# High and low parts of the weights word by word in one array, on one core of a Trainium2 chip

## The chip, the cores and the metric

The kernel runs on 1 core of one Trainium2 chip. The metric is the device time in microseconds of one execution on that core, as the median of several runs. Less is better.

## What is computed

The reference is two transformer blocks in float32, one after the other, on 256 tokens of width 1024. The first block also reads 256 context tokens; the second adds 16 meta tokens in front. Cut to what matters:

```python
# first block
px = modulate(rms_norm(x, g_pre_mix), sh_m, sc_m) @ w_in        # x: 256 x 1024, w_in: 1024 x 2320
pc = modulate(rms_norm(ctx, g_pre_mix), csh_m, csc_m) @ w_in
mixed = concat(attention(...), mlstm_output(...))               # window attention and a two-way mLSTM
x = x + gt_m * rms_norm(mixed @ w_out, g_post_mix)
x = x + gt_f * rms_norm(swiglu(modulate(rms_norm(x, g_pre_ffn), sh_f, sc_f), w_ffn_in, w_ffn_out), g_post_ffn)
# second block, h = [16 meta tokens, x]
h = h + 0.5 * swiglu_2(rmsnorm(h, ffn1_norm), ffn1_w_gate, ffn1_w_up, ffn1_w_down)     # hidden width 2816
u = rmsnorm(h, mix_norm) @ w_in_2                                                      # attention, GLA, gates
h = h + (sigmoid(gate_a) * (ya @ w_branch_att) + sigmoid(gate_b) * (yb @ w_branch_gla)) @ w_out_2
h = h + 0.5 * swiglu_2(rmsnorm(h, ffn2_norm), ffn2_w_gate, ffn2_w_up, ffn2_w_down)
out = rmsnorm(h, final_norm)[:, 16:]
```

Nearly all of the arithmetic is products of a weight matrix with 256, 258, 272 or 512 token columns.

## The kernel before

Every weight tile comes from HBM in float32 and is used in two parts, a high one rounded to the matmul type `F32R` and a low one that is the rest. A product then takes three matmuls: high weight times high activation, high weight times low activation, low weight times high activation (`split_mm`, lines 2003 to 2007, and copies of it at 2134, 2203 to 2205 and 2398).

The weights run through a ring of four slots (`RING` = 4). Each slot holds up to 1408 words in every partition (`SLOT`); most tiles are 1024 words (four row blocks of 256 columns), those of the down projections 1408 (eleven row blocks of 128 columns). Three arrays of four slots stand next to each other: `raw` takes the transfer from HBM, which SyncE issues (line 419); ScalarE copies `raw` to `hi` (line 621); VectorE subtracts, `lo = raw - hi` (line 1143); TensorE reads `hi` and `lo`. The order of the slots is fixed: ScalarE waits for TensorE's count of finished slots (`mm_done`) before it overwrites `hi`, VectorE waits for ScalarE, TensorE for VectorE, and SyncE's next transfer into `raw` for VectorE. All of this runs a slot or more ahead of TensorE.

```python
hi = sbuf(root, "hi", [P, RING, SLOT], F32R)                                                  # 137
lo = sbuf(root, "lo", [P, RING, SLOT], F32R)                                                  # 138
act.activation(hi[:, j, 0:width], raw[:, j, 0:width], ACT.Copy).then_inc(hi_ready, 1)         # 621
dve.tensor_tensor(lo[:, j, 0:width], raw[:, j, 0:width], hi[:, j, 0:width].bitcast(F32), ...) # 1143
pe.matmul(out_, wH, xH, start=start, stop=False)                                              # 2005
pe.matmul(out_, wH, xL, start=False, stop=False)                                              # 2006
return pe.matmul(out_, wL, xH, start=False, stop=stop)                                        # 2007
pe.matmul(out_, n5H[:, k, rows], hi[:, k // 2, w], start=k == 0, stop=False)                  # 2203
pe.matmul(out_, n5H[:, k, rows], lo[:, k // 2, w], start=False, stop=False)                   # 2204
return pe.matmul(out_, n5L[:, k, rows], hi[:, k // 2, w], start=False, stop=k == KD - 1)      # 2205
pe.matmul(bank, hi[:, 0, 0:P], hi[:, 0, 0:512], start=True, stop=True)                        # 2480
```

In `pe.matmul(out, a, b)` the second argument is the stationary operand, which a separate LDWEIGHTS instruction (PEld in the profile) brings into the array; the third is the moving operand, which streams past it, one column per clock at best. So the weights are stationary in `split_mm`: 128 words of `hi` or `lo` for each LDWEIGHTS. They are the moving operand in two places only. One is `by_token` (lines 2203 to 2205), used for the mLSTM's values and output gates (phases `winv` and `wino` of the first block): 48 calls of three matmuls, each with 512 words of `hi` or `lo` moving, 12 matmuls to a piece; the pieces are laid between the steps of the attention (`scores`, `probabilities`, `values_out`). The other is `keep_clock` (line 2480), which multiplies to no purpose while TensorE waits for a norm: 7 matmuls before `gu0`, 16 before `gu1`, 4 and 3 at the end of the kernel, each with 512 words of `hi` moving.

The phases in order: `win0`, `winq`, `winm`, `winv`, `wino` (products with `w_in`, beside attention and mLSTM), `wout`, `gu0` and `dn0` (first feed-forward, 11 and 4 turns of four slots), `gu1` and `dn1`, `in2k` and `in2g`, `brb` and `bra`, `wout2`, `gu2` and `dn2`. TensorE, VectorE, ScalarE and SyncE run a turn of the feed-forwards in hardware loops.

Of the kernel before, what the change touches and what calls it, by code (L numbers as in the profile page):

```python
# [7 lines left out]
F32R = mybir.dt.float32r  # L8
# [6 lines left out]
P = 128  # L15
# [13 lines left out]
SLOT = HALF * P  # L29
RING = 4  # L30
# [84 lines left out]
def program(nc, dr, out):  # L115
    with ExitStack() as root:
        def sbuf(stack, name, shape, dt=F32):
            return stack.enter_context(nc.sbuf_tensor(name, shape, dt))
# [15 lines left out]
        slabs1 = ExitStack()  # L134
        slab_hi = sbuf(slabs1, "slab_hi", [P, RING, SLOT])
        slabs1.close()
        hi = sbuf(root, "hi", [P, RING, SLOT], F32R)
        lo = sbuf(root, "lo", [P, RING, SLOT], F32R)
        sinkn = sbuf(root, "sinkn", [P, 16])
        negm = sbuf(root, "negm", [P, 32])  # L140
        staged = ExitStack()
# [2653 lines left out]
```

## Time and profile before

| | us |
|---|---|
| median of 3 runs | 971.9 (969.46 to 973.7) |
| the profiled execution's own time | 973.39 |
| span of the profiled execution | 971.6 |
| TensorE (matmul) busy | 956.6, 98% of the span |
| weight load (PEld) busy | 888.0, 91% |
| VectorE busy | 641.1, 66% |
| ScalarE busy | 495.0, 51% |

The span runs from the first to the last instruction on the chip; the execution's own time has some 2 us more around it. A matmul's duration in the profile includes its passage through the array, and matmuls overlap: what one costs TensorE is the distance from its start to the next start, which is shorter than its duration. The same holds for weight loads. The mean granted clock of TensorE is 0.994 of full speed.

### The profile page before, as it was taken

What the parts mean: (1) busy time and instruction counts of PE and PEld (TensorE: products, weight loads), DVE (VectorE), ACT (ScalarE), POOL (GpSimd) and SP (SyncE); (2) the same over time, 40 slices, a digit from 0 to 9 for tenths busy, and PEclk for the clock granted to TensorE, in tenths of its full rate; (3) what the DMA queues carried; (4) which work ended last, traced back from release to release, by engine and by line L of the source; (5) the groups of instructions that cost most, each with busy time, mean ns of one, the idle gap of its engine ahead of it and who ended that gap; (6) DMA issues with size and microseconds to landing.
All of it is one profiled execution on the core that took longest, in us unless ns stands there. A gap on an engine that the chain in (4) does not pass through costs nothing.

```text
span 971.6 us, 19403 instructions
## 1 busy us (share of the span) xinstructions
PE 956.6 (98%) x7543; PEld 888.0 (91%) x7543; DVE 641.1 (66%) x990; ACT 495.0 (51%) x762; POOL 66.6 (7%) x100
## 2 busy tenths in 40 slices
PE   8999999999999999999999999999999999999997
PEld 3776778899999999899999999999999999999997
DVE  4788886687666765765555546665778766665654
ACT  3755647655444544554444434645566555444540
POOL 0012002200000021000000000200210100000000
PEclk9999998999999999999999999999999999999999
DMA  9982447547556696266666844663445566667841
GB/s 346 384 283 88 131 131 231 163 172 216 173 174 182 191 308 177 71 197 173 176 177 183 217 119 129 212 188 108 131 131 173 154 194 204 184 177 220 217 120 43
DMA packets 189183, 176.06 MB, mean 181 GB/s; under 512 B 7312, under 2 KB 177824, under 8 KB 188752
## 3 DMA queue, kind: packets, MB, share of 16 engines
q1 hardware_dynamic: 183456, 154.29, 53.9%
q0 software_dynamic: 4960, 17.64, 5.3%
q10 hardware_dynamic: 720, 3.49, 0.9%
q8 instruction: 31, 0.51, 0.2%
q14 instruction: 16, 0.13, 0.0%
HBM read 174.32 MB, written 1.05 MB: 180 GB/s over the span
## 4 chain that ended last, share of the span: by engine, by line
PE 87%; DVE 8%; ACT 2%; issue 1%; DMA 1%; POOL 0%; DVEq 0%; ACTq 0%; POOLq 0%
PE acc L2005 23%; PE acc L2006 23%; PE acc L2007 23%; PE acc L2398 3%; DVE lo L1143 2%; PE acc L2101 1%; DMA stage<-in_w_late 1%; PE acc L2203 1%; PE acc L2205 1%; PE acc L2204 1%; PE wk L2064 1%; PE wk L2005 1%; PE wk L2006 1%; PE wk L2007 1%; PE wk L2134 1%
## 5 line engine op out<-in xcount | busy, mean ns | idle before, releaser
L1143 DVE TENSOR_TENSOR lo<-raw,hi 128x1024 fp32r<-128x1024 f32 (+1 forms) x259 | 331.5, 1291 | 208.0 <-ACT hi L621 207.7
L621 ACT ACTIVATE hi<-raw 128x1024 fp32r<-128x1024 f32 (+1 forms) x260 | 283.8, 1099 | 133.5 <-PE acc L2007 114.7
L2005 PE MATMUL acc<-n_high,hi 128*128 128x272 f32 (+3 forms) x1016 | 290.5, 286 | 0.5 <-DVE hbuf L1671 0.3
L2006 PE MATMUL acc<-n_low,hi 128*128 128x272 f32 (+3 forms) x1016 | 289.2, 285 | 0.0
L2007 PE MATMUL acc<-n_high,lo 128*128 128x272 f32 (+3 forms) x1016 | 288.1, 284 | 0.0
L2005 PEld LDWEIGHTS acc<-n_high,hi 128*128 128x128 f32 (+1 forms) x1016 | 191.4, 188 | 3.1 <-issue 1.4
L2006 PEld LDWEIGHTS acc<-n_low,hi 128*128 128x128 f32 (+1 forms) x1016 | 191.0, 188 | 0.5
L2007 PEld LDWEIGHTS acc<-n_high,lo 128*128 128x128 f32 (+1 forms) x1016 | 191.0, 188 | 0.2
L2005 PE MATMUL acc<-g_high,hi 128*128 128x256 f32 (+1 forms) x528 | 148.9, 282 | 0.9 <-DVE lo L1143 0.9
L2006 PE MATMUL acc<-g_low,hi 128*128 128x256 f32 (+1 forms) x528 | 149.1, 282 | 0.0
L2007 PE MATMUL acc<-g_high,lo 128*128 128x256 f32 (+1 forms) x528 | 148.7, 282 | 0.0
L2005 PE MATMUL acc<-mixH,hi 128*128 128x256 f32 x400 | 112.9, 282 | 0.5 <-DVE gab L1844 0.4
L2006 PE MATMUL acc<-mixL,hi 128*128 128x256 f32 x400 | 112.1, 280 | 0.0
L2007 PE MATMUL acc<-mixH,lo 128*128 128x256 f32 x400 | 112.1, 280 | 0.0
L2005 PEld LDWEIGHTS acc<-g_high,hi 128*128 128x128 f32 x528 | 99.3, 188 | 1.2 <-DVE lo L1143 1.1
L2007 PEld LDWEIGHTS acc<-g_high,lo 128*128 128x128 f32 x528 | 99.9, 189 | 0.0
L2006 PEld LDWEIGHTS acc<-g_low,hi 128*128 128x128 f32 x528 | 99.1, 188 | 0.0
L2006 PEld LDWEIGHTS acc<-mixL,hi 128*128 128x128 f32 x400 | 76.5, 191 | 0.0
L2005 PEld LDWEIGHTS acc<-mixH,hi 128*128 128x128 f32 x400 | 75.1, 188 | 1.5 <-DVE gab L1844 0.7
L2007 PEld LDWEIGHTS acc<-mixH,lo 128*128 128x128 f32 x400 | 75.1, 188 | 0.0
L566 POOL TENSOR_TENSOR sq<-sq 128x256 f32<-128x256 f32 (+1 forms) x28 | 23.8, 851 | 482.7 <-ACT sq L923 431.0
L923 ACT ACTIVATE sq<-R (+3 forms) x36 | 15.9, 441 | 57.6 <-DVE R L1715 49.9
(424 smaller groups left out, 1254.5 us busy)
## 6 DMA issues: line engine op xcount, KB each, us to landing
raw<-in_w_in SPq DMA_DIRECT2D x52, 512.0 KB, 3.8
raw<-in_w_ffn_in SPq DMA_DIRECT2D x44, 512.0 KB, 3.9
raw<-in_ffn_w_gate SPq DMA_DIRECT2D x44, 512.0 KB, 3.9
raw<-in_ffn_w_up SPq DMA_DIRECT2D x44, 512.0 KB, 3.8
raw<-in_ffn_w_down SPq DMA_DIRECT2D x32, 704.0 KB, 4.8
stage<-in_w_late POOLq DMA_DIRECT2D x24, 512.0 KB, 5.4
raw<-in_w_ffn_out SPq DMA_DIRECT2D x16, 704.0 KB, 6.2
raw<-in_w_out SPq DMA_DIRECT2D x16, 512.0 KB, 3.6
```

What stands on the lines that cost most here:

```text
L566: ins = pool.tensor_tensor(sq[:, 0, 0:width], sq[:, 0, 0:width], sq[:, k, 0:width], ALU.add)
L621: act.activation(hi[:, j, 0:width], raw[:, j, 0:width], ACT.Copy).then_inc(hi_ready, 1)
L923: act.activation(sq[:, k, 0:width], R[:, k, t0:t0 + width], ACT.Square).then_inc(sq_ready, 1)
L1143: dve.tensor_tensor(lo[:, j, 0:width], raw[:, j, 0:width], hi[:, j, 0:width].bitcast(F32), ALU.subtract).then_inc(lo_ready, 1)
L2005: pe.matmul(out_, wH, xH, start=start, stop=False)
L2006: pe.matmul(out_, wH, xL, start=False, stop=False)
L2007: return pe.matmul(out_, wL, xH, start=False, stop=stop)
L2064: ins = pe.matmul(SLAB_BANK[n][32 * kk:32 * kk + 32, :], silu_c[:, 4 * q + kk, :], SLAB_MEM[n][2 * q + kk // 2][:, 512 * (kk % 2):512 * (k ...
L2101: pe.matmul(acc[:, 0, 0:width], cink[:, 0, 0, 0:P], cink.rearrange("p a b t -> p (a b t)")[:, 0:width], start=True, stop=True)
L2134: ins = pe.matmul(bank[:, T * m:T * m + T], ws[:, j, w], xs[:, k, 0:T], start=k == 0 and m == 0 and n == 0, stop=k == KD - 1 and n == 2, s ...
L2203: pe.matmul(out_, n5H[:, k, rows], hi[:, k // 2, w], start=k == 0, stop=False)
L2398: ins = pe.matmul(out_, ws[:, j, w], xs[:, k, :], start=k == 0 and m == 0 and n == 0, stop=k == KD - 1 and n == 2, skip_group_check=True)
```

## The change

The two arrays `hi` and `lo` are replaced by one of the same total size in which the words alternate: high, low, high, low. The names `hi` and `lo` become views of it, so every read and write of either steps over two words (8 bytes) where it took adjacent words (4 bytes) before. No instruction, semaphore or transfer is added, removed or moved, and `raw` stays as it is. The arrays allocated after these two keep their addresses. `slab_hi` (line 135), a temporary array that lies where `hi` begins, now lies under the high and low words of slots 0 and 1 and no longer under the high words of all four.

```diff
@@ -134,8 +134,8 @@
         slabs1 = ExitStack()
         slab_hi = sbuf(slabs1, "slab_hi", [P, RING, SLOT])
         slabs1.close()
-        hi = sbuf(root, "hi", [P, RING, SLOT], F32R)
-        lo = sbuf(root, "lo", [P, RING, SLOT], F32R)
+        weights = sbuf(root, "weights", [P, RING, SLOT, 2], F32R)
+        hi, lo = weights[:, :, :, 0], weights[:, :, :, 1]
         sinkn = sbuf(root, "sinkn", [P, 16])
         negm = sbuf(root, "negm", [P, 32])
         staged = ExitStack()
```

## Rows read from the trace of the kernel before

**Rows 1.** The page: span, busy time by engine, slices of the span
```profile
span 971.6 us, 19403 instructions
PE 956.6 (98%) x7543; PEld 888.0 (91%) x7543; DVE 641.1 (66%) x990; ACT 495.0 (51%) x762; POOL 66.6 (7%) x100
...
PEclk9999998999999999999999999999999999999999
```

**Rows 2.** The chain that ended last, whole span, shares by line
```profile
by line: PE acc L2005 23.2%; PE acc L2006 22.9%; PE acc L2007 22.8%; PE acc L2398 2.6%; DVE lo L1143 1.6%; issue 1.3%; PE acc L2101 1.1%; DMA stage<-in_w_late 1.0%; PE acc L2203 1.0%; PE acc L2205 0.9%; PE acc L2204 0.9%; PE wk L2064 0.8%; 
```

**Rows 3.** Groups by line and shape: splits (count, busy us, mean ns, idle before)
```profile
L1143 DVE TENSOR_TENSOR lo<-raw,hi 128x1024 fp32r<-128x1024 f32 x207 | 252.3, 1229 | 153.0 <-ACT hi L621 152.8
L621 ACT ACTIVATE hi<-raw 128x1024 fp32r<-128x1024 f32 x208 | 217.2, 1051 | 86.8 <-PE acc L2007 84.6 <-DMA raw<-in_w_in 1.8
...
L1143 DVE TENSOR_TENSOR lo<-raw,hi 128x1408 fp32r<-128x1408 f32 x48 | 77.9, 1634 | 54.3 <-ACT hi L621 54.2
...
L621 ACT ACTIVATE hi<-raw 128x1408 fp32r<-128x1408 f32 x48 | 65.7, 1375 | 46.7 <-PE acc L2007 30.1 <-DMA raw<-in_w_ffn_out 12.5 <-DMA raw<-in_ffn_w_down 3.7
```

**Rows 4.** Line 2005's weight loads: duration min/median/max; 16 and 128 words
```profile
L2005 PEld LDWEIGHTS acc<-g_high,hi x528: 186/188/190, 329.0 to 961.7; 128*128 128x128 f32 x176
...
L2005 PEld LDWEIGHTS wk<-n5H,hi x8: 92/94/98, 65.6 to 70.2; 128*16 128x16 f32 x8
```

**Rows 5.** Timeline of TensorE: start and duration us, 512 moving words of weights
```profile
105.20 0.39 PE L2203 MATMUL acc<-hi,n5H 128*128 128x512 f32 x1
105.43 0.40 PE L2204 MATMUL acc<-lo,n5H 128*128 128x512 f32 x1
...
107.07 0.40 PE L2205 MATMUL acc<-hi,n5L 128*128 128x512 f32 x1
```

**Rows 6.** The same in `dn0` and `dn2`: 256 moving words of activations
```profile
350.04 0.28 PE L2005 MATMUL acc<-g_high,hi 128*128 128x256 f32 x1
...
351.40 0.28 PE L2005 MATMUL acc<-g_high,hi 128*128 128x256 f32 x1
...
899.91 0.28 PE L2005 MATMUL acc<-g_high,hi 128*128 128x256 f32 x1
...
900.97 0.28 PE L2005 MATMUL acc<-g_high,hi 128*128 128x256 f32 x1
```

**Rows 7.** Groups of TensorE from 89.8 to 145.5 us
```profile
L2203 PE MATMUL acc<-hi,n5H 128*128 128x512 f32 x48 | 20.1, 419 | 0.0
L2205 PE MATMUL acc<-hi,n5L 128*128 128x512 f32 x48 | 18.9, 395 | 0.0
L2204 PE MATMUL acc<-lo,n5H 128*128 128x512 f32 x48 | 18.9, 394 | 0.0
L2254 PE MATMUL wk<-cst,Sm 128*128 128x128 f32 x48 | 7.0, 279 | 0.5 <-DVE Sm L1446 0.4
```

**Rows 8.** Windows: busy us of each engine (instructions), granted clock, DMA
```profile
89.80:100.60 10.80, 10.80 (x73) 8.05 (x70) 10.55 (x27) 3.93 (x8) 0.46 (x2) 1.00 0.17 51
100.60:144.90 44.30, 43.82 (x249) 31.64 (x249) 36.09 (x78) 25.78 (x49) 4.25 (x12) 1.00 0.45 143
```

**Rows 9.** Timeline around `keep_clock` before `gu0`, before `gu1`, at the end
```profile
197.38 1.86 PE L2480 MATMUL acc<-hi 128*128 128x512 f32 x7
...
199.57 0.36 PE L2005 MATMUL wk<-n_high,hi 128*128 128x258 f32 x1 [0.33 <-DVE n_low L1647]
...
391.15 4.00 PE L2480 MATMUL acc<-hi 128*128 128x512 f32 x16
...
395.99 0.37 PE L2005 MATMUL wk<-n_high,hi 128*128 128x272 f32 x1 [0.84 <-DVE n_low L1647]
...
962.55 1.17 PE L2480 MATMUL acc<-hi 128*128 128x512 f32 x4
...
963.85 0.61 PE L2738 MATMUL wk<-cst,sq 128*128 128x1 f32 x4
...
964.31 0.94 PE L2480 MATMUL acc<-hi 128*128 128x512 f32 x3
...
965.43 0.70 PE L2742 MATMUL wk<-xg,cst 128*128 128x256 f32 x2 [0.18 <-DVE xg L1990]
```

**Rows 10.** Windows, columns as in rows 8: a turn of `gu0`, of `gu1`
```profile
228.50:240.10 11.60, 11.60 (x98) 11.60 (x98) 8.16 (x13) 5.54 (x8) 0.00 (x0) 1.00 0.66 206
...
460.00:472.00 12.00, 12.00 (x98) 12.00 (x98) 6.90 (x7) 5.43 (x8) 0.00 (x0) 1.00 0.64 175
```

**Rows 11.** Groups by shape: TensorE's matmuls with a stationary `hi`, by moving words
```profile
L2005 PE MATMUL acc<-n_high,hi 128*128 128x272 f32 x400 | 115.0, 287 | 0.3 <-DVE hbuf L1671 0.3
L2005 PE MATMUL acc<-mixH,hi 128*128 128x256 f32 x400 | 112.9, 282 | 0.5 <-DVE gab L1844 0.4
L2005 PE MATMUL acc<-g_high,hi 128*128 128x256 f32 x352 | 98.2, 279 | 0.9 <-DVE lo L1143 0.9
L2005 PE MATMUL acc<-n_high,hi 128*128 128x258 f32 x336 | 95.4, 284 | 0.0
...
L2005 PE MATMUL acc<-n_high,hi 128*128 128x256 f32 x272 | 77.6, 285 | 0.3 <-DVE n_low L1956 0.3
```

## The prediction

> **What bounds the kernel now.** I read the page first: TensorE is busy 956.6 of 971.6 us at a granted clock of 0.9 or more in every slice [rows 1]. VectorE at 66% and ScalarE at 51% have room on average. The chain that ended last says the same: lines 2005 to 2007 hold 69% of it, while VectorE's split of the weights holds 1.6% [rows 2]. So what the change does to TensorE's reads counts first, and what it does to the two splitting engines counts only once they run late.
>
> The change touches nothing but the distance between words, so the next thing to read is how fast each engine takes words today. Four readers or writers of `hi` and `lo` are concerned.
> - TensorE's moving stream: eight steps of 512 words take 107.07 - 105.20 = 1.87 us, 234 ns each [rows 5]. That is 0.457 ns per word, or 8.8 bytes per ns in every partition. At 2.4 GHz the array itself would want 213 ns, so the stream runs 10% behind it although TensorE waits for nothing there. With 256 words, 12 steps of `dn0` take 1.36 us, 113 ns each, and 9 of `dn2` take 1.06 us, 118 ns each [rows 6]: 0.44 to 0.46 ns per word again. A turn of `gu0` is 96 matmuls of 258 words in 11.6 us, 121 ns each, one of `gu1` 96 of 272 words in 12.0 us, 125 ns each [rows 10].
> - The weight load: 188 ns for 128 words, 94 ns for 16 words [rows 4], so 94 / 112 = 0.84 ns per word; 128 words occupy it for 107 ns, 4.8 bytes per ns.
> - ScalarE's split: (1375 - 1051) / 384 = 0.84 ns per word [rows 3].
> - VectorE's split: (1634 - 1229) / 384 = 1.05 ns per word [rows 3].
>
> **The change part by part.** No row of this trace shows an operand with a step of two words. I therefore compare the stretch of memory that each stream sweeps per ns with the fastest sweep that a row shows, 8.8 bytes per ns, that of the moving stream. Stepped by 8 bytes, VectorE's streams sweep 8 / 1.05 = 7.6 bytes per ns, below it; the weight load and ScalarE sweep 8 / 0.84 = 9.5, 8% above it; the moving stream would have to sweep 17.7, twice it. By this measure three of the four keep their pace or nearly so, and the fourth cannot be promised to.
>
> (a) Moving reads of 512 weight words in `by_token`. There are 3 x 48 = 144 of them [rows 7]. Bounds: nothing, if a stepped read costs the same; 234 ns each, if 512 words with gaps cost what 1024 adjacent words would (256 to 512 words adds 234 - 116 = 118 ns [rows 5, 6], so another 512 words add some 236). I take the upper end, because this stream is the only one that moves two words in the time of one weight-load word, and it already runs behind the clock. Sum: 144 x 234 = 33.7 us. Does it land? From 89.8 to 144.9 us TensorE is busy 10.80 + 43.82 of 55.1 us [rows 8], and its only wait for another engine is 0.4 us for a softmax step at line 2254 [rows 7]. TensorE works in order, so these matmuls push all that follows: 33.3 us land. The chain gives lines 2203 to 2205 2.8%, 27 us [rows 2]; the missing 6 us belong to 90 to 104 us, where VectorE is 98% busy [rows 8] and the chain runs through it. That cover is used up: with TensorE's pieces 2.8 us longer each, VectorE's steps fit in them. Below nothing: I see no reason for a gain here.
>
> (b) Moving reads in `keep_clock`, 30 matmuls, doubled to 468 ns. Before `gu0` 7 x 234 = 1.6 us start at 197.38 and end near 199.0; the next product waits for VectorE until 199.57 [rows 9]. Doubled they end near 200.6, 1.1 us late. Before `gu1` 16 x 234 = 3.7 us end near 394.9 and become 7.5, ending near 398.6 where 395.99 was the start: 2.6 us late, of which the later waits of that front may give back some; I take 2. At the end 4 become 1.87 us and end at 964.4, 0.55 us after 963.85; then 3 of 468 ns end at 966.3, where line 2742 would start at 965.43 + 0.55: 0.3 more. Together 1.1 + 2 + 0.85 = 4 us; bounds 0 and 4.6.
>
> (c) Weight loads from `hi` and `lo`. Lines 2005 to 2007 have 2016 loads of 128 words each (the sum of their groups, of which the largest stand in [rows 11]), lines 2134 and 2398 another 336: about 6,400. A load overlaps the matmul before it; it occupies 107 ns where starts are 113 to 125 ns apart. If it holds its 0.84 ns per word, nothing changes. If it is held to the sweep of 8.8 bytes per ns, it takes 128 x 8 / 8.8 = 116 ns, and with the 6 ns that now lie between load and pace in `dn0`, 122 ns. The 256-word matmuls at 113 to 118 ns would then go at 122 (+4 to 9 ns, some 3,400 of them), those of 258 words from 121 to 122, those of 272 words not at all: about 22 us. Upper bound: each word costs like two, 188 + 107 = 295 ns of duration and 214 ns of occupation, so starts 220 ns apart, +100 ns x 6,400 = 640 us. I take nothing, because the load is within 8% of a sweep that the rows show, and keep 22 us for the range.
>
> (d) The splits. If stepped words cost them nothing: 0. If each cost like two: VectorE 1.05 x 1024 = +1.07 us, ScalarE +0.86 us. In a turn of `gu0` VectorE has 8.16 of 11.6 us of work and four splits [rows 10]: 8.16 + 4.3 = 12.4, just over the turn; in `gu1` 6.90 + 4.3 = 11.2 of 12.0 fits. On the chain VectorE's splits have 1.6%, 15.5 us or some 13 splits [rows 2, 3]: 13 x 1.07 = 14 us, and 11 turns of `gu0` add up to 9 us. Today's cover in the loops is the idle time before the splits, 153 us before VectorE's [rows 3]. I take nothing: 7.6 bytes per ns lies below the shown sweep, and ScalarE's 8% more (0.07 us a split) is hidden by that idle time.
>
> (e) Addresses: the sum of the sizes is the same, so what is allocated behind keeps its place, and the one transfer that lands there (`slab_hi`, before the first split) keeps its waits. Nothing.
>
> Sum against the profiled execution: 973.4 + 33.3 + 4 = 1010.7 us; that execution lies 1.5 us above the median, so against the median 971.9 + 37 = **1009 us**.
>
> **The skill against the rows.** The rows show one word per 0.457 ns moving and one per 0.84 ns loading [rows 4, 5], both of adjacent words, and decide nothing on steps. The Trainium skill, page "Advanced Engine Details and Errata", section "SBUF Cachelines", says that accesses get full performance as long as at least two fall on a 16-byte line. Two words of a view that steps by 8 bytes do; by that rule all of (a) to (d) is nothing and the time stays at 972, which is the first rival. Against it the page "Vector Engine (DVE) Microarchitecture Reference", section 5.2, asks for runs of two adjacent words and gives about 1.7 ns per word where there are none; by that VectorE's split would take 0.65 ns more per word, toward the last two rivals. Its table tells of steps other than two words, so neither rule is shown here.
>
> **The rivals.**
> - Not slower, 972 us: the memory hands TensorE a piece wide enough that every second word of it still feeds one word per 0.45 ns. Place: lines 2203 to 2205. Price: none. It decides if starts stay 234 ns apart; any stretch above 240 ns speaks against it. For it: the 9% lag behind the array is there with stationary weights too, and may have nothing to do with reading.
> - Weight loads just too slow as well, 1009 + 22 = 1031 us, from (c). For it: the load has 6 to 11 ns of slack and must sweep 8% faster than anything shown.
> - Every stepped word costs like two: 1009 + 640 = about 1650 us, and TensorE is bound by its loads. For it: the upper bounds above; against it: three of the four sweeps stay near a shown one.
> - Only the splits suffer, TensorE not: 972 + 14 + 9 = 995 us at most.
> - Faster: equal products in `dn0` and `dn2` differ by 4.4 ns [rows 6], for a reason the rows don't show. If another order of words made all 256-word matmuls go at 113 ns and those of 258 words at 114, 1,600 x 4.4 + 1,056 x 6.6 ns = 14 us would go: 958 us.
> - That the change does nothing of what it says is excluded for the reads: the views are stepped. A stepped operand may be built into the same instructions, as a step is part of each operand.
>
> **How the numbers follow.** Moving stream doubled, rest unchanged: 0.42. Not slower: 0.27. Loads just too slow: 0.12. Everything doubled: 0.12. Splits alone: 0.03. Faster: 0.04. The likeliest gives 1009. The range takes in the unchanged case from below, 968, and the case of the slower loads with room for twice its size above 1009, 1060; the doubled case and the faster one, 0.16, stay out. About 0.5%, 5 us, is what a measurement here can tell from no change. Faster by more 0.04; within 0.27; slower by more 0.42 + 0.12 + 0.12 + 0.03 = 0.69.
>
> **What would show it.** Right: starts near 468 ns apart at lines 2203 to 2205, their stretch 33 us longer, `keep_clock` of 16 taking 7.5 us; weight loads at 188 ns and starts in `gu0`, `gu1` and `dn2` at 121, 125 and 118 ns; splits at 1.05 and 1.23 us. Wrong: starts still at 234 ns, or weight loads above 200 ns with the whole feed-forward stretched, or a VectorE split near 1.9 us.

## The result, and the profile after

The changed kernel takes 1019.0 us (median of 4 runs, 1018.2 to 1021.3) against 971.5 us before (four runs; the three that stood ahead of the prediction had 971.9): a ratio of 1.0503, 95% interval 1.0478 to 1.0529, so 47.6 us slower. The forecast was 1009 us in a range of 968 to 1060. Its direction and range held; 10 of the 47.6 us were missing from the likeliest case.

The page of the changed kernel, beside [rows 1], and its chain by line, beside [rows 2] (both of the arrays are called `weights` now):

```profile
span 1019.5 us, 19403 instructions
PE 1007.2 (99%) x7543; PEld 908.6 (89%) x7543; DVE 641.1 (63%) x990; ACT 519.3 (51%) x762; POOL 68.0 (7%) x100
...
by line: PE acc L2005 23.8%; PE acc L2007 23.1%; PE acc L2006 23.0%; PE acc L2398 2.5%; PE acc L2203 2.3%; PE acc L2205 2.1%; PE acc L2204 2.1%; PE acc L2480 1.4%; DMA slab_hi<-in_w_ada 1.1%; PE wk L2005 0.8%; PE wk L2007 0.8%; PE wk L2006 
```

The same 19403 instructions, and the chain's new time lies in TensorE's lines. Lines 2203 to 2205, where weights are the moving operand, went from 2.8% to 6.5% of the chain; `keep_clock` (line 2480) has appeared with 1.4%; VectorE's busy time is to the tenth what it was. Its splits, 1.6% of the chain before, no longer stand among the chain's largest lines. That TensorE is now late enough to cover them is how I read it.

The timeline of TensorE at the end of `wino` (start and duration in us), beside [rows 5]:

```profile
173.45 0.65 PE L2205 MATMUL acc<-weights,n5L 128*128 128x512 f32 x1
173.90 0.65 PE L2203 MATMUL acc<-weights,n5H 128*128 128x512 f32 x1
174.36 0.65 PE L2204 MATMUL acc<-weights,n5H 128*128 128x512 f32 x1
174.81 0.64 PE L2205 MATMUL acc<-weights,n5L 128*128 128x512 f32 x1
175.38 1.10 PE L2359 MATMUL acc<-vtok,kw 128*64 128x129 f32 x16
```

512 moving words now take 1.36 / 3 = 453 ns from start to start, where they took 234. In `dn0`, beside [rows 6], the moving operand is still adjacent words of activations and only the stationary one is stepped:

```profile
381.82 0.28 PE L2005 MATMUL acc<-g_high,weights 128*128 128x256 f32 x1
...
383.26 0.28 PE L2005 MATMUL acc<-g_high,weights 128*128 128x256 f32 x1
```

12 steps in 1.44 us: 120 ns each instead of 113. Not doubled, but 7 ns more, in a place where nothing but TensorE's own pace counts. The weight loads beside [rows 4] and the splits beside [rows 3]:

```profile
L2005 PEld LDWEIGHTS acc<-g_high,weights x528: 193/193/202, 362.3 to 1008.9; 128*128 128x128 f32 x176
...
L1143 DVE TENSOR_TENSOR weights<-raw,weights 128x1024 fp32r<-128x1024 f32 x207 | 252.2, 1229 | 166.4 <-ACT weights L621 165.9
L621 ACT ACTIVATE weights<-raw 128x1024 fp32r<-128x1024 f32 x208 | 235.8, 1147 | 82.9 <-PE acc L2007 80.4 <-DMA raw<-in_w_in 2.3
...
L621 ACT ACTIVATE weights<-raw 128x1408 fp32r<-128x1408 f32 x48 | 72.2, 1511 | 44.6 <-PE acc L2007 31.2 <-DMA raw<-in_w_ffn_out 9.8 <-DMA raw<-in_ffn_w_down 3.2
```

A load takes 193 to 196 ns instead of 188; ScalarE's split of 1024 words 1147 ns instead of 1051; VectorE's split, which now reads and writes stepped words, takes 1229 ns as before.

To see where the 47.6 us arose I set the start of the same matmul in both traces side by side (the n-th of the 7543 that each trace holds) and took the growth of the difference over each stretch:

| stretch of the program | later by, us |
|---|---|
| up to the first piece of `winv` | -0.4 |
| `winv` and `wino` | +30.4 |
| from there to `keep_clock` before `gu0` (mostly `wout`) | +1.2 |
| `keep_clock` of 7, 16 and 4 + 3 matmuls | +1.0, +2.6, +0.8 |
| `gu0` and `dn0` | +4.5 |
| `gu1` and `dn1` | -0.5 |
| `in2k` to the end of the attention of the second block | +3.5 |
| from there through `dn2` | +5.0 |

So three terms: moving reads in `winv` and `wino` 30.4, `keep_clock` 4.4, and 13 to 14 us spread over all products with stationary weights. The last is the one that the forecast had at nothing. In `gu0`, with 258 moving words, 800 matmuls lose 0.9 us, 1.1 ns each; in `gu2` and `dn2`, with 256, 1,200 lose 2.6 us, 2.2 ns each.

### The profile page after: what moved, and what is told of

Read it like the earlier page. It is cut to its first block, busy times and chain, and to the rows that moved or that the text cites. A ratio compares the mean times of both kernels' runs of the same rounds, so it can differ in the third digit from the quotient of the medians.

```text
span 1019.5 us, 19403 instructions
## 1 busy us (share of the span) xinstructions
PE 1007.2 (99%) x7543; PEld 908.6 (89%) x7543; DVE 641.1 (63%) x990; ACT 519.3 (51%) x762; POOL 68.0 (7%) x100
## 3 DMA queue, kind: packets, MB, share of 16 engines
HBM read 174.32 MB, written 1.05 MB: 172 GB/s over the span
## 4 chain that ended last, share of the span: by engine, by line
PE 93%; DVE 3%; ACT 1%; DMA 1%; issue 1%; SPq 0%; DVEq 0%; ACTq 0%
PE acc L2005 24%; PE acc L2007 23%; PE acc L2006 23%; PE acc L2398 3%; PE acc L2203 2%; PE acc L2205 2%; PE acc L2204 2%; PE acc L2480 1%; DMA slab_hi<-in_w_ada 1%; PE wk L2005 1%; PE wk L2007 1%; PE wk L2006 1%; PE wk L2246 1%; PE acc L2134 1%; PE wk L2268 1%
## 5 line engine op out<-in xcount | busy, mean ns | idle before, releaser
L1143 DVE TENSOR_TENSOR weights<-raw,weights 128x1024 fp32r<-128x1024 f32 (+1 forms) x259 | 331.7, 1291 | 225.5 <-ACT weights L621 225.1
L621 ACT ACTIVATE weights<-raw 128x1024 fp32r<-128x1024 f32 (+1 forms) x260 | 308.9, 1201 | 127.4 <-PE acc L2007 111.6
L2005 PE MATMUL acc<-n_high,weights 128*128 128x272 f32 (+3 forms) x1016 | 293.8, 289 | 0.4 <-DVE hbuf L1671 0.4
L2006 PE MATMUL acc<-n_low,weights 128*128 128x272 f32 (+3 forms) x1016 | 289.9, 285 | 0.0
L2007 PE MATMUL acc<-n_high,weights 128*128 128x272 f32 (+3 forms) x1016 | 289.8, 285 | 0.0
L2005 PEld LDWEIGHTS acc<-n_high,weights 128*128 128x128 f32 (+1 forms) x1016 | 198.4, 195 | 2.7 <-issue 1.4
L2006 PEld LDWEIGHTS acc<-n_low,weights 128*128 128x128 f32 (+1 forms) x1016 | 198.4, 195 | 0.4
L2007 PEld LDWEIGHTS acc<-n_high,weights 128*128 128x128 f32 (+1 forms) x1016 | 197.9, 195 | 0.2
L2005 PE MATMUL acc<-g_high,weights 128*128 128x256 f32 (+1 forms) x528 | 150.6, 285 | 0.7 <-DVE weights L1143 0.7
L2007 PE MATMUL acc<-g_high,weights 128*128 128x256 f32 (+1 forms) x528 | 150.2, 285 | 0.0
L2005 PE MATMUL acc<-mixH,weights 128*128 128x256 f32 x400 | 113.9, 285 | 0.5 <-DVE gab L1844 0.5
L2007 PE MATMUL acc<-mixH,weights 128*128 128x256 f32 x400 | 113.0, 283 | 0.0
L2005 PEld LDWEIGHTS acc<-g_high,weights 128*128 128x128 f32 x528 | 102.4, 194 | 0.9 <-DVE weights L1143 0.9
L2007 PEld LDWEIGHTS acc<-g_high,weights 128*128 128x128 f32 x528 | 102.6, 194 | 0.0
L2005 PEld LDWEIGHTS acc<-mixH,weights 128*128 128x128 f32 x400 | 77.3, 193 | 1.3 <-DVE gab L1844 0.7
L2007 PEld LDWEIGHTS acc<-mixH,weights 128*128 128x128 f32 x400 | 77.6, 194 | 0.0
```

## The experiments

The theory going in: the step between words costs, once for each kind of read, and the kinds add up. The rivals: it is not the step but the place (high and low parts of a slot close together, so that engines meet in the same memory), or the slower splits of ScalarE, and not TensorE's own reads. The code cuts below show the lines that matter; like edits of other lines are left out.

**One array without a step.** In each slot first all high words, then all low ones. `Words(array, part, g)` is a view of one part (0 high, 1 low): with `g` None the parts lie one behind the other, with a number they alternate in runs of `g` words:

```diff
-        hi = sbuf(root, "hi", [P, RING, SLOT], F32R)
-        lo = sbuf(root, "lo", [P, RING, SLOT], F32R)
+        weights = sbuf(root, "weights", [P, RING, 2 * SLOT], F32R)
+        hi, lo = Words(weights, 0, None), Words(weights, 1, None)
```

> One array again, as in the change, but in each slot first all high words and then all low words, so that every view steps by one word. Theory 1, the step is what costs: the time is that of the kernel before, 971 us within 3, loads 188 ns, 512 moving words 234 ns apart, ScalarE's split of 1024 words 1.05 us. Theory 2, it is the place (high and low parts of a slot close together, so that engines meet in the same stretch of memory): it stays well above 971, up to 1019 us. Theory 3: an array with the slots side by side changes the 113 or 118 ns between starts of equal products: up to 14 us faster.

Measured: 970.5 us against 970.2, ratio 1.0002 (0.9981 to 1.0023). High and low parts share one slot's stretch of memory as in the change, the addresses of everything else are the same, and nothing is lost. So the place is not the cause at the scale of a slot; the runs of four words below, where the parts lie 16 bytes apart, say the same of small distances for the moving reads. What remains is the step. Nor was anything gained. All later layouts are built on this one.

**The moving reads put back**, first those of `winv` and `wino`, then those of `keep_clock` too. The split and `by_token` take their words from the layout without a step in these phases:

```diff
+        hi, lo = Words(weights, 0, 1), Words(weights, 1, 1); hiT, loT = Words(weights, 0, None), Words(weights, 1, None)
-                act.activation(hi[:, j, 0:width], raw[:, j, 0:width], ACT.Copy).then_inc(hi_ready, 1)
+                act.activation((hiT if isinstance(g, int) and g in (BASE["winv"], BASE["wino"]) else hi)[:, j, 0:width], raw[:, j, 0:width], ACT.Copy).then_inc(hi_ready, 1)
-                pe.matmul(out_, n5H[:, k, rows], hi[:, k // 2, w], start=k == 0, stop=False)
+                pe.matmul(out_, n5H[:, k, rows], hiT[:, k // 2, w], start=k == 0, stop=False)
```

and, in the second kernel only,

```diff
-                    pe.matmul(bank, hi[:, 0, 0:P], hi[:, 0, 0:512], start=True, stop=True)
+                    pe.matmul(bank, weights[:, 0, 0:P], weights[:, 0, 0:512], start=True, stop=True)
```

> The change, but in the phases winv and wino alone (mLSTM values and output gates, where weights are the moving operand) the slots hold all high words and then all low ones. Theory 1: starts at lines 2203 to 2205 are 234 ns apart again and the 30.5 us which the change lost between 90 and 145 us come back: 1019 - 30.5 = 988.5 us; the weight loads elsewhere stay at 195 ns. If those 30 us were lost to the slower splits or to VectorE's and ScalarE's steps of the attention beside it, little comes back in spite of 234 ns.

> As the one before, and keep_clock reads adjacent words too, so that only weight loads and splits step by two words. Theory 1: keep_clock gives back 4 to 5 us: 984 us. The remaining 12 us are those of the weight loads: starts in dn0 stay near 120 ns, in gu0 122, in dn2 120. If keep_clock's length is hidden by the norm beside it: 988 us as before.

Measured: 989.4 us, ratio 1.0194 (1.0163 to 1.0225), and 986.8 us, ratio 1.0164 (1.0131 to 1.0196). The first gives back 1019.0 - 989.4 = 29.6 us where 30.5 was expected; in its trace lines 2203 to 2205 start 232 ns apart again in the middle, and `winv` and `wino` are 30.4 us shorter than in the change. Their splits are without a step here too; that these are not what gave the time back shows in the kernel with stepped splits alone, below. The second gives 2.6 us more where I had 4 to 5. In the traces, `keep_clock` costs the first kernel 1.1 + 2.6 + 0.7 = 4.4 us against the kernel before and the second nothing, so the medians and the traces agree only within their spread of some 2 us. What is left, 16 us with 13 to 19 in its interval (13.2 in the trace), has no stepped moving read in it.

**The prices alone.** A kernel that does nothing of the reference's work but copy an input, and runs each spacing by itself: 16 matmuls with 512 moving words from an array with one stationary operand of adjacent words, then 24 matmuls each with stepped stationary words, then ScalarE and VectorE alone.

> None of the reference's work but the copy of an input: each price alone. 16 matmuls of 512 moving words for each spacing (every word, every 2nd, 3rd, 4th, 8th, and runs of 2, 4, 8, 16 words with as many left out), 24 matmuls of 256 and of 128 moving words for each spacing of the 128 stationary words (1, 2, 3, 4, 8), then ScalarE and VectorE alone with 1024 words. Theory 1a, memory is read in pieces of 16 bytes at one rate: moving 512 words take 230, 455, 680, 900, 900 ns; runs of 2 take 455 like every 2nd word, runs of 4, 8 and 16 take 230. Theory 1b, pieces of 8 bytes: 230, 455, 455, 455, 455, and runs of 2 take 230 already. Loads with every word or every 2nd take 107 to 114 ns of TensorE's time, with every 4th word and above about 225 by theory 1a, 114 by 1b. ScalarE's write of every 2nd word: 0.94 ns per word as in the kernel, every 4th 1.8 by theory 1a. VectorE: 1.05 ns up to every 2nd word, every 4th 1.7 to 1.8 by theory 1a, 1.05 by 1b.

Its timeline of TensorE, each line one spacing; the price of one is the distance to the start of the next line by the count. Lines 124 to 132: every word, every 2nd, 3rd, 4th, 8th as moving operand; 134 and 136: runs of 2 and of 4 words with as many left out. Line 150: every 8th of the stationary words beside 256 moving words. Lines 152 to 158: 128 stationary words, every one, every 2nd, 3rd, 4th, beside 128 moving words.

```profile
30.11 3.79 PE L124 MATMUL acc<-mov,sta 128*128 128x512 f32 x16
33.73 7.41 PE L126 MATMUL acc<-mov,sta 128*128 128x512 f32 x16
40.97 7.38 PE L128 MATMUL acc<-mov,sta 128*128 128x512 f32 x16
48.16 7.57 PE L130 MATMUL acc<-mov,sta 128*128 128x512 f32 x16
55.54 7.08 PE L132 MATMUL acc<-mov,sta 128*128 128x512 f32 x16
62.44 7.40 PE L134 MATMUL acc<-mov,sta 128*128 128x512 f32 x16
69.66 3.91 PE L136 MATMUL acc<-mov,sta 128*128 128x512 f32 x16
73.41 3.89 PE L138 MATMUL acc<-mov,sta 128*128 128x512 f32 x16
...
96.50 5.96 PE L150 MATMUL acc<-mov,sta 128*128 128x256 f32 x24
102.29 2.79 PE L152 MATMUL acc<-mov,sta 128*128 128x128 f32 x24
104.92 2.99 PE L154 MATMUL acc<-mov,sta 128*128 128x128 f32 x24
107.75 4.32 PE L156 MATMUL acc<-mov,sta 128*128 128x128 f32 x24
111.91 5.82 PE L158 MATMUL acc<-mov,sta 128*128 128x128 f32 x24
117.52 5.78 PE L160 MATMUL acc<-mov,sta 128*128 128x256 f32 x24
```

Moving: 3.62 / 16 = 226 ns for adjacent words, then 452, 449, 461, 431 for every 2nd, 3rd, 4th and 8th, 451 for runs of 2, and 3.75 / 16 = 234 for runs of 4. Both forms of theory 1 fall for the moving operand. By pieces of 16 bytes at one rate every 3rd and 4th word should have cost 680 and 900; by pieces of 8 bytes runs of 2 should have been free. It has two prices only: 0.44 to 0.46 ns per word in runs of four, 0.84 to 0.90 otherwise, however far apart.

Loads: with 128 moving words TensorE has less to stream than to load, so these are the loads' own prices: 2.63 / 24 = 110 ns for adjacent words, 118 for every 2nd, 173 for every 3rd, 234 for every 4th. That is 64, 96 and 128 pieces of 16 bytes at 1.84, 1.81 and 1.83 ns each: here the 16-byte theory holds to 2%, and a step of two words is the last one that costs next to nothing. Every 8th word takes 5.79 / 24 = 241 ns, as much as every 4th to 3%: what counts is the number of pieces and not the stretch swept, by which it would have doubled.

ScalarE (lines 58 to 67: writing every word, every 2nd, 3rd, 4th; 70: every 8th) and VectorE (93 and 96: reading `hi` at every word and every 2nd; 99: every 4th; 111: reading and writing every 2nd), columns: count, busy us, mean ns, idle before:

```profile
L70 ACT ACTIVATE dst<-src 128x1024 fp32r<-128x1024 f32 x4 | 8.1, 2032 | 0.1
...
L67 ACT ACTIVATE dst<-src 128x1024 fp32r<-128x1024 f32 x4 | 8.0, 1998 | 0.1
...
L64 ACT ACTIVATE dst<-src 128x1024 fp32r<-128x1024 f32 x4 | 6.2, 1552 | 0.1
...
L61 ACT ACTIVATE dst<-src 128x1024 fp32r<-128x1024 f32 x4 | 4.5, 1116 | 0.1
...
L58 ACT ACTIVATE dst<-src 128x1024 fp32r<-128x1024 f32 x4 | 4.2, 1056 | 106.8 <-PE acc L162 106.7
...
L99 DVE TENSOR_TENSOR dst<-src,mov 128x1024 fp32r<-128x1024 f32 x4 | 7.9, 1971 | 0.1
...
L111 DVE TENSOR_TENSOR dst<-src,mov 128x1024 fp32r<-128x1024 f32 x4 | 4.9, 1226 | 0.1
L96 DVE TENSOR_TENSOR dst<-src,mov 128x1024 fp32r<-128x1024 f32 x4 | 4.9, 1226 | 0.1
L93 DVE TENSOR_TENSOR dst<-src,mov 128x1024 fp32r<-128x1024 f32 x4 | 4.9, 1225 | 175.5 <-ACT dst L84 175.4
```

The same 1.8 ns: with the 187 ns that [rows 3] leave beside 0.84 ns per word, ScalarE's 1116, 1552 and 1998 are 929 / 512, 1365 / 768 and 1811 / 1024 = 1.81, 1.78 and 1.77 ns per piece, and every 8th word costs what every 4th does (2032 ns). VectorE needs 2 x 1.05 = 2.1 ns for two words anyway, which is longer than a piece, which fits that every 2nd word costs it nothing, read and written. The Trainium skill, page "Advanced Engine Details and Errata", section "SBUF Cachelines", asks for two accesses to a 16-byte line; for VectorE, and nearly for the loads and ScalarE, the trace agrees (1226 ns against 1225, 118 against 110, 1116 against 1056). For the moving operand it does not: 452 ns against 226, with two words on every line.

**Loads alone and splits alone.** Two complements settle who owns the remaining 13 to 16 us. In the first, splits write adjacent words and TensorE's loads step by two over them; in the second, splits write every second word and TensorE reads adjacent ones. Both so multiply mixed words. `Load` and `Split` are views for reading and for writing, and the number behind each is its step:

```diff
+        hi, lo, hiW, loW, hiM, loM = (f(weights, q, s) for f, s in ((Load, 2), (Split, 1), (Load, 1)) for q in range(2))
-                act.activation(hi[:, j, 0:width], raw[:, j, 0:width], ACT.Copy).then_inc(hi_ready, 1)
+                act.activation(hiW[:, j, 0:width], raw[:, j, 0:width], ACT.Copy).then_inc(hi_ready, 1)
```

and `(Load, 1), (Split, 2)` in the other.

> Splits write adjacent words (all high ones, then all low ones), moving reads of weights take adjacent words, and only the weight loads step by two words; they so take a mixture of high and low words, and the products with stationary weights are not those of the reference. Theory 1, the 13 to 16 us that remained when the moving reads were put back are those of the loads: 985 to 987 us, starts in dn0 at 120 ns, weight loads at 193 to 196 ns. Theory 2, they come from the splits (ScalarE's write of a split 0.1 us longer, or engines meeting in memory): 971 us and loads at 188 ns.

> The counterpart: ScalarE and VectorE write every second word as in the change, and TensorE reads adjacent words everywhere, stationary and moving (so again mixed words, and other products). Theory 1: 971 us within 3, although ScalarE's split of 1024 words takes 1.15 us instead of 1.05, since VectorE waits for it with time to spare. Theory 2: up to 987 us.

Measured: loads stepped 986.0 us, ratio 1.0136 (1.0108 to 1.0164); splits stepped 971.5 us, ratio 0.9990 (0.9973 to 1.0006), both against 972.7 us in the same series. In the first, 256-word matmuls of `dn0` and `dn2` start 120 ns apart as in the change. From the groups by shape, first of the kernel with stepped loads, then of that with stepped splits:

```profile
L621 ACT ACTIVATE weights<-raw 128x1024 fp32r<-128x1024 f32 x208 | 217.1, 1052 | 94.1 <-PE acc L2007 91.2 <-DMA raw<-in_w_in 2.4
...
L2005 PEld LDWEIGHTS acc<-n_high,weights 128*128 128x128 f32 x1008 | 197.5, 196 | 2.4 <-issue 1.4 <-DVE hbuf L1671 0.5
```

```profile
L1143 DVE TENSOR_TENSOR weights<-raw,weights 128x1024 fp32r<-128x1024 f32 x207 | 252.4, 1229 | 155.4 <-ACT weights L621 154.9
L621 ACT ACTIVATE weights<-raw 128x1024 fp32r<-128x1024 f32 x208 | 233.5, 1136 | 77.3 <-PE acc L2007 74.8 <-DMA raw<-in_w_in 1.8 <-DMA raw<-in_ffn_w_up 0.6
L2005 PEld LDWEIGHTS acc<-n_high,weights 128*128 128x128 f32 x1008 | 190.6, 189 | 3.0 <-issue 1.4 <-DVE hbuf L1671 0.6 <-DVE n_low L1956 0.5
```

ScalarE at 1052 ns and loads at 196: 13 us slower. ScalarE at 1136 ns and loads at 189: not slower. The remainder belongs to the loads. ScalarE's 85 ns more per split are hidden whole: VectorE's idle time before its splits, 153 us before, is 155 us, and the total does not move. The stepped splits of `winv` and `wino` are among them, so those phases' 30 us are not theirs either.

**Moving reads alone, in single words, in runs of four and in runs of two.** High words and then low ones everywhere but in `winv` and `wino`, and there the parts alternate one by one, four by four, or two by two (the cut is that of four by four):

```diff
+        hi, lo = Words(weights, 0, None), Words(weights, 1, None); hiT, loT = Words(weights, 0, 4), Words(weights, 1, 4)
```

> High words and then low words in every slot but those of the phases winv and wino, where they alternate one by one; keep_clock takes adjacent words. If the losses add up independently: 971 + 30 = 1001 us, starts at lines 2203 to 2205 near 450 ns, weight loads at 188 ns and dn0 at 113 or 118 ns. If the moving reads cost less when the loads are fast: under 995.

> The same, but in winv and wino the parts alternate in runs of four words (16 bytes high, 16 bytes low). The prices measured alone say 233 ns for 512 words in runs of four with four left out: 971 us within 3. If what counts is the stretch of memory swept (8 KB for 2 KB of words, as with every second word): 1001 us.

> As the kernel with runs of four words in winv and wino, but in runs of two (8 bytes high, 8 bytes low). The prices measured alone say 451 ns for 512 words in runs of two, like every second word, and 233 ns in runs of four. So it should be as slow as with single words: 1001 to 1005 us. If two adjacent words were enough for the moving stream: 972 us.

Measured: single words 1004.8 us, ratio 1.0321 (1.0290 to 1.0351); runs of four 972.3 us, ratio 0.9991 (0.9970 to 1.0011); runs of two 1002.3 us, ratio 1.0302 (1.0258 to 1.0347). The timeline of TensorE with runs of four, then with runs of two:

```profile
105.28 0.39 PE L2204 MATMUL acc<-weights,n5H 128*128 128x512 f32 x1
...
106.67 0.40 PE L2204 MATMUL acc<-weights,n5H 128*128 128x512 f32 x1
```

```profile
105.36 0.64 PE L2204 MATMUL acc<-weights,n5H 128*128 128x512 f32 x1
105.81 0.63 PE L2205 MATMUL acc<-weights,n5L 128*128 128x512 f32 x1
...
106.72 0.63 PE L2204 MATMUL acc<-weights,n5H 128*128 128x512 f32 x1
```

1.39 / 6 = 232 ns against 1.36 / 3 = 453. Both sweep 4096 bytes for 2048 bytes of words (not the 8 KB that the expectation has), and one of them costs nothing: the stretch of memory swept is not what is paid for.

**More prices.** Does a run have to fill an aligned piece, and does a stepped load show beside every width of moving operand?

> Prices alone again, none of the reference's work but the copy of an input. Moving words: runs of four starting at a multiple of 16 bytes take 233 ns; starting 8 or 4 bytes later, 450 ns if a run has to fill one aligned piece of 16 bytes, 233 ns if only its length counts; runs of six of eight between the two (504 words, 340 ns); 512 adjacent words starting 4 or 8 bytes late 227 to 234 ns. Weight loads of adjacent and of every second word beside 256, 258, 272 and 512 moving words: with adjacent words 113 to 121, 114 to 121, 120 to 125 and 234 ns; with every second word 120, 120 to 122, 125 and 234 ns, no matter whether the first word is even (the high part) or odd (the low part): the load is the longer of the two up to 256 or 258 words and hidden above. ScalarE writes every second word at 0.85 to 0.9 ns, (1408 against 1024 words), the 0.94 ns of the kernel then being the meeting of engines.

Its timeline of TensorE. Lines 96, 98 and 100: runs of four of eight words, starting at a multiple of 16 bytes, 8 bytes late, 4 bytes late. 102: runs of six of eight (504 words). 104: runs of eight of sixteen, 8 bytes late. 106: 512 adjacent words, 4 bytes late. 110, 112 and 114: loads of adjacent words, of every 2nd and of every 2nd from an odd word on, beside 256 moving words; from line 116 on the same beside 258, then 272 and 512, of which the cut shows the first.

```profile
29.53 3.86 PE L96 MATMUL acc<-mov,sta 128*128 128x512 f32 x16
33.23 7.41 PE L98 MATMUL acc<-mov,sta 128*128 128x512 f32 x16
40.46 7.43 PE L100 MATMUL acc<-mov,sta 128*128 128x512 f32 x16
47.69 4.95 PE L102 MATMUL acc<-mov,sta 128*128 128x504 f32 x16
52.47 5.40 PE L104 MATMUL acc<-mov,sta 128*128 128x512 f32 x16
57.70 3.97 PE L106 MATMUL acc<-mov,sta 128*128 128x512 f32 x16
61.51 3.90 PE L108 MATMUL acc<-mov,sta 128*128 128x512 f32 x16
65.24 5.80 PE L110 MATMUL acc<-mov,sta 128*128 128x256 f32 x48
70.88 5.96 PE L112 MATMUL acc<-mov,sta 128*128 128x256 f32 x48
76.67 5.96 PE L114 MATMUL acc<-mov,sta 128*128 128x256 f32 x48
82.47 5.92 PE L116 MATMUL acc<-mov,sta 128*128 128x258 f32 x48
```

Runs of four: 231 ns aligned, 452 ns when they start 8 or 4 bytes late. Runs of six of eight: 4.78 / 16 = 299 ns. That is one aligned piece of four words at 1.8 ns and two single words at 0.88 each, 3.56 ns for six words, times 84 = 299: the two prices mix word by word. The expectation had 340 ns for it. Runs of eight starting 8 bytes late hold one aligned piece and four single words: the same sum gives 64 x (1.8 + 4 x 0.88) = 340 ns, and they took 327, which fits less well; the expectation had nothing on them. Adjacent words that start 4 bytes late lose next to nothing (238 ns).

Stepped loads beside 256 moving words cost 5.79 / 48 = 120.6 ns against 117.5 with adjacent ones (in the first kernel of prices 120.0 against 119.2); beside 258 and 272 words the same reading of the start times gives 121.7 against 120.0 and 125.2 against 125.4; beside 512 words 232 both. An odd first word (the low part) makes no difference: 5.80 / 48 = 120.8. So a stepped load gives 120 to 121 ns everywhere, and what it costs depends on the pace it finds: 113 ns in `dn0`, 118 in `dn2`, 117 to 119 here. ScalarE alone writes every second word at (1462 - 1115) / 384 = 0.90 ns, at the upper end of what was expected; in the kernel it is 0.95. The expectation puts the rest down to the meeting with other engines; no run separates that, so it stays open.

## Why the prediction was right, and where it fell short

- **What bounds the kernel**: right. TensorE is busy 99% of the longer span, and nearly all of the time lost is in the distance between its starts. One reading was off: the granted clock was not 0.9 or more in every slice of [rows 1], the seventh slice has an 8. Nothing in the sum rests on it.
- **(a) Moving reads in `by_token`, 33.3 us**: 30.4 in the traces, 29.6 when they alone were put back, 32 when they alone were stepped. The price was put at 234 ns more for each and measured at 453 - 234 = 219. The size was right, its reason was not, and that the size came out is in part luck: at a step of two words the stretch swept and the number of words taken singly give the same doubling. The argument went by the stretch swept per ns; runs of four sweep the same stretch for nothing, and every 4th word, which sweeps twice as much again, costs no more than every 2nd. The prices fit a stream that takes four words at once from a full aligned piece of 16 bytes and otherwise one at a time, at twice the price per word.
- **(b) `keep_clock`, 4 us**: 1.0, 2.6 and 0.8 us for the three places, against 1.1, 2 and 0.85.
- **(c) Weight loads, taken at nothing**: this step failed. They cost 13 us with nothing else stepped. Its own second case nearly had the price, 116 ns of occupation for a load that must keep to 8.8 bytes per ns: 118 ns measured, and 16 bytes per 1.82 ns are 8.8 bytes per ns. Its reason holds up to every 4th word and fails at every 8th, where 241 ns sweep 17 bytes per ns: pieces count, and not the sweep. The reason given for nothing, that the load is within 8% of a shown sweep, does not follow: 8% of a load is 8 to 11 ns (118 against the 110 measured alone or the 107 worked out), and the prediction's own slack in `dn0` was 6 ns. The case was priced at 22 us since it put all 256-word matmuls at 122 ns; they went to 120, so that stretches already at 118 (`gu2`, `dn2`) lost 2 ns and not 4, and 258 words 1 ns, 272 words less than 1. In the two traces, 47.9 us apart, the loads' 13 to 14 us and the 0.4 that (b) had too little, minus the 2.9 that (a) had too much, are the 10.6 us that the forecast's 37.3 lacks; in the medians it is 10.
- **(d) The splits, nothing**: right, shown by stepping them alone (0.9990). VectorE's price did not move at all (1229 ns), and the 0.65 ns more per word that the prediction quotes against its first rival did not come. ScalarE's rose by 96 ns where 70 was worked out; with the 85 ns of the stepped splits alone nothing was lost.
- **(e) Addresses, nothing**: right, shown by the array without a step (1.0002).
- **The rivals.** Not slower: decided against by the starts of lines 2203 to 2205, 453 ns. Loads just too slow: true as a mechanism, at 1031 us 12 too high. Everything doubled: false; it would need a step of four words, where a load alone takes 234 ns. Splits alone: false (0.9990). Faster: nothing of it; the 113 and 118 ns stretches changed places in the array without a step (`dn0` at 118, `dn2` at 113) and left the time where it was. Why a stretch runs at one or the other stays open.

## What to carry to other kernels

When a layout spaces out what TensorE reads, ask first which operand it is. The moving operand in this 4-byte type wants full aligned runs of four words and pays double for anything less; the stationary operand, ScalarE and VectorE pay by the 16-byte piece, 1.8 ns each, so two of four words are nearly free and one of four is not. If two parts must share an array, alternating them in runs of four words cost the moving reads nothing where single words cost 32 us. An array in runs of four for the weight loads as well was not run. A small price that falls on the pacing operation 6,400 times is not small: 2 ns each on average are 13 us here.

## What the runs showed of the hardware

- One 16-byte piece per 1.8 ns is a common price: weight loads 1.81 to 1.84, ScalarE's writes 1.77 to 1.81, VectorE reading every 4th word (1971 - 150) / 1024 = 1.78, where 150 ns is what [rows 3] leave beside 1.05 ns per word. Adjacent moving words go at 1.8 ns for four words too, 0.44 to 0.46 ns each, 6 to 10% more than one clock of the 2.4 GHz level, 0.417 ns.
- Not expected: a moving operand of scattered words never cost more than 0.9 ns per word, even with every word on a piece of its own, which is half of what a load pays there.
- The granted clock had no part in it. It was 1.00 from 89.3 to 174.8 us of the changed kernel, through all of the slow matmuls. In the first kernel of prices it was 0.50, the 1.2 GHz level, from 113 to 122 us; it fell while loads of every 4th word paced TensorE. The prices of stepped words stayed what they were: loads of every 4th word 234 ns at either level (lines 148 and 158), and 256 moving words, every 2nd one, 229 ns at 0.50 (line 160) and 230 at 1.00 (line 162).
